# A hybrid attention, retention and mixture-of-experts layer: constants on the sync engine's queue, a twelfth weight buffer, x loaded first, two narrow rounding buffers for the last units, and the last 8 MB of weights by columns

## The reference

```python
h = rms_norm(x, norm1_g)
proj = h @ w_in                        # 2048 x 6736: q, k, v, index q/k/w, retention q/k/v/gate
attn_out = dsa_attention(...)          # an index score picks 64 keys a query, softmax over them
ret_out = silu(rg) * rms_norm(retention(rotate(rq), rotate(rk), rv))
x = x + concatenate([attn_out, ret_out]) @ w_out          # 2048 x 2048
h = rms_norm(x, norm2_g)
# router: the best of 4 groups, in it the best 2 of 8 experts, weights comb
a, b = h @ w1[e], h @ w3[e]            # for each of 32 experts, 2048 x 512
y = (silu(a) * b * comb[e]) @ w2[e]    # 512 x 2048
x = x + sum over e of y
```

## Time and profile before

| | |
|---|---|
| median of three runs | 1363.29 us |
| the profiled execution | 1364.37 us, of it 1362.5 us from the first to the last instruction |
| mean granted TensorE clock | 0.865 |
| TensorE busy | 985.4 us (72%) |
| VectorE, ScalarE, GpSimd busy | 330.6, 306.6, 80.0 us |
| moved by DMA | 480.69 MB, 353 GB/s over the span |
| chain that ended last | DMA 48%, TensorE 47%, VectorE 2% |

### The profile page before, as it was taken

How to read it: one execution, slowest core, us unless ns; L and a number is a source line. 1 busy time by engine, 2 the same in 40 slices (tenths; PEclk the granted TensorE clock), 3 DMA queues, 4 the chain that set the end, 5 groups by cost and what they waited for, 6 DMA issues and landing times.

```text
span 1362.5 us, 18965 instructions
## 1 busy us (share of the span) xinstructions
PE 985.4 (72%) x8264; PEld 654.3 (48%) x8264; DVE 330.6 (24%) x504; ACT 306.6 (23%) x553; POOL 80.0 (6%) x61
## 2 busy tenths in 40 slices
PE   7999999999999875556566365547736563674547
PEld 6987887888888651324234133313413421342222
DVE  5457967544753200010010000001001000100101
ACT  6545555555543310001001000100100010010000
POOL 1000242500110020000000000000000000000000
PEclk9999999999999888778787777888878777986888
DMA  8744644544596999999999999999999999999997
GB/s 278 231 153 158 213 145 137 183 164 147 192 411 237 405 426 435 430 426 431 432 432 425 436 431 427 433 431 433 424 435 432 426 434 432 429 425 435 430 423 305
DMA packets 61412, 480.69 MB, mean 353 GB/s; under 512 B 3816, under 2 KB 8096, under 8 KB 43952
## 3 DMA queue, kind: packets, MB, share of 16 engines
q1 hardware_dynamic: 60832, 478.89, 85.9%
q0 software_dynamic: 528, 1.06, 0.3%
HBM read 477.84 MB, written 2.10 MB: 352 GB/s over the span
## 4 chain that ended last, share of the span: by engine, by line
DMA 48%; PE 47%; DVE 2%; SPq 1%; issue 1%; ACT 1%; ACTq 0%
DMA ring<-w_dram 48%; PE ps L1559 11%; PE ps L1304 9%; PE ps L1306 9%; PE ps L1305 9%; PE ps L1597 5%; DVE w_lo L854 1%; PE ps L1514 1%; PE ps L1320 1%; DMA xs<-x_dram 1%; SPq L393 1%; PE ps L1661 1%; PE ps L1414 0%; PE ps L1336 0%; SPq L400 0%
## 5 line engine op out<-in xcount | busy, mean ns | idle before, releaser
L1559 PE MATMUL ps<-ring,side_buf 128*32 128x256 f32 x4000 | 273.5, 438 | 252.3 <-DMA ring<-w_dram 252.3
L1559 PEld LDWEIGHTS ps<-ring,side_buf 128*32 128x32 f32 x4000 | 155.9, 126 | 372.9 <-issue 316.1
L1304 PE MATMUL ps<-w_hi,zT_half 128*128 128x512 f32 (+2 forms) x576 | 221.7, 385 | 1.7 <-DVE w_lo L854 1.7
L1306 PE MATMUL ps<-w_hi,zT_half 128*128 128x512 f32 (+2 forms) x576 | 218.6, 379 | 0.0
L1305 PE MATMUL ps<-w_lo,zT_half 128*128 128x512 f32 (+2 forms) x576 | 218.5, 379 | 0.0
L854 DVE TENSOR_TENSOR w_lo<-raw_buf,w_hi 128x1024 fp32r<-128x1024 f32 (+2 forms) x144 | 182.0, 1281 | 142.7 <-ACT w_hi L574 142.0
L1597 PE MATMUL ps<-ring,side_buf 128*32 128x512 f32 x960 | 129.6, 701 | 97.5 <-DMA ring<-w_dram 97.2
L574 ACT CAST w_hi<-raw_buf 128x1024 fp32r<-128x1024 f32 (+2 forms) x144 | 143.6, 1016 | 107.5 <-PE ps L1306 101.4
L1230 DVE TENSOR_TENSOR xs<-xs,ps 128x512 f32<-128x512 f32 x56 | 38.5, 688 | 487.8 <-PE ps L1526 487.7
L792 ACT ACTIVATE side_buf<-ps,st 128x256 f32<-128x256 f32 x16 | 6.7, 470 | 554.2 <-PE ps L1559 554.2
L1597 PEld LDWEIGHTS ps<-ring,side_buf 128*32 128x32 f32 x960 | 35.8, 127 | 186.0 <-issue 179.5
(11 more groups left out here) (192 smaller groups left out, 501.3 us busy)
## 6 DMA issues: line engine op xcount, KB each, us to landing
ring<-w_dram SPq DMA_DIRECT2D x56, 4096.0 KB, 25.1
ring<-w_dram SPq DMA_DIRECT2D x73, 2048.0 KB, 21.4
raw_buf<-w_in_dram SPq DMA_DIRECT2D x48, 1024.0 KB, 5.0
raw_buf<-w_out_dram SPq DMA_DIRECT2D x16, 1024.0 KB, 6.0
spare<-w_dram SPq DMA_DIRECT2D x2, 2048.0 KB, 13.1
ring<-w_dram SPq DMA_DIRECT2D x4, 1024.0 KB, 14.0
ring<-w_dram SPq DMA_DIRECT2D x8, 512.0 KB, 17.4
raw_buf<-w_in_dram SPq DMA_DIRECT2D x4, 608.0 KB, 6.2
```

What stands on the lines that cost most here:

```text
L1304: mm(b, zhi(c)[:, t], wh, start=(c == 0), stop=False)
L1306: last = mm(b, zlo(c)[:, t], wh, start=False, stop=(c == C - 1))
L1559: last = mm(ps[part, up, pair * WIDE:(pair + 1) * WIDE], h_e[:, c, slots], w[m][:, cc * NB + h * WIDE:cc * NB + (h + 1) * WIDE], start=(c ...
```

## The change

- The gains, the constants and the router's weights are loaded by SP on its own queue: the first at q = 5, the router's at q = 63 behind a wait for `ret_ready`. GpSimd issues no DMA any more, and the 16 KB a partition that its queue had are a new tile `place`, a fourth extra buffer. It takes chunk 11 at q = 40.
- x: three of its four parts are loaded ahead of the first weights, and the first 1 MB of weights comes in two halves, with the last part of x between them. ScalarE and VectorE split one piece of x more ahead of the first unit.
- From unit 136 on (NARROW) only two slots of rounded weights are used, and a rounding waits for the unit before the last. The first spare area lies over the other two slots and takes chunk 9 when unit 135 has been used. The order of the loads behind the last raw weights changes, since `first_slot` does.
- The squares of block 2 move behind the last `copy_zT`; the sum of the squares moves behind `sel`; three products of 128 x 512 are added in front of the wait for `sel_ready`.
- The last four chunks come by columns: both rows of the left half, then each row of the right half. The left half is scattered ahead of the right half's products.

The diff, cut:

```diff
+NARROW = UNITS - 8
-RING, EXTRA = 8, 3
+RING, EXTRA = 8, 4
-LAST_PIECES = [(0, 0, 4), (1, 0, 2), (1, 2, 2)]
+LAST_PIECES = [(0, 2, 0, 2), (0, 1, 2, 2), (1, 1, 2, 2)]
+        w_split = nc.alloc_sbuf_tensor_at("w_split", [P, 8192], F32R, offset=side)
+        W_HI, W_LO = (4096, 0), (6144, 2048)
+        spare = [nc.alloc_sbuf_tensor_at(f"spare{i}", [P, 4096], F32, offset=side + 4 * 6144 * i) for i in range(2)]
+        place = sb("place", [P, 4096])
-        extra = [xs_flat, spare[0], spare[1]]
+        extra = [xs_flat, spare[0], spare[1], place[:, :]]
+        def split_slot(u):
+            return u % SPLIT if u < NARROW else u % 2
+        def split(part, u):
+            at = part[split_slot(u) // 2] + split_slot(u) % 2 * 1024
+            return w_split[:, at:at + 2 * unit(u)[2]]
@@ sync
-                if q == 1:
-                    for i in range(1, X_PARTS):
-                        load_x(i)
+                if q == 5:
+                    for dst, src in ((gain_q, q_norm_g), (gain_k, k_norm_g), (ln_w, idx_k_ln_w), (ln_b, idx_k_ln_b)):
+                        sp.dma_start(dst, src.partition_broadcast(P).rearrange("p l n -> p (l n)")).then_inc(gains_in, 16)
+                    sp.dma_start(gr_rows[:, :], ret_norm_g.rearrange("l (h d) -> (l h) d", d=HD)).then_inc(ret_gain_in, 16)
+                    sp.dma_start(const[:, P:CONSTS], consts[:, P:CONSTS]).then_inc(const_in, 16)
+                if q == 40:
+                    load_first(11)
+                if q == 63:
+                    sp.wait_ge(ret_ready, 2)
+                    sp.dma_start(g2_col[:, :], norm2_g.rearrange("l (p c) -> p (l c)", c=C)).then_inc(g2_in, 16)
...
+                    for g in range(GROUPS):
+                        sp.dma_start(stage_r[:, g].rearrange("p (q n) -> p q n", q=4),
+                                     w_router[0, g].rearrange("(q p c) e -> p q (c e)", q=4, c=4)).then_inc(router_in, 16)
+                if q == 0:
+                    load_x(1)
+                    load_x(2)
+                    sp.dma_start(at[:, 0:2 * n].rearrange("p (c n) -> p c n", c=2),
+                                 src[:, c:c + 2, col:col + n]).then_inc(raw_first, 16)
+                    load_x(3)
+                    sp.dma_start(at[:, 2 * n:4 * n].rearrange("p (c n) -> p c n", c=2),
+                                 src[:, c + 2:c + 4, col:col + n]).then_inc(raw_landed[0], 16)
...
+            sp.wait_ge(unit_used, NARROW)
+            load_first(9)
             sp.wait_ge(lo_done, UNITS - 4)
+            load_first(0)
+            sp.wait_ge(unit_used, UNITS - 4)
+            load_first(2)
+            sp.wait_ge(lo_done, UNITS)
             load_first(1)
-            sp.wait_ge(unit_used, UNITS - 4)
+            sp.wait_ge(unit_used, UNITS)
             load_first(3)
-            sp.wait_ge(lo_done, UNITS)
-            load_first(2)
-            sp.wait_ge(unit_used, UNITS)
-            load_first(4)
-            load_first(9)
             sp.wait_ge(logits_done, TH)
             sp.wait_ge(ssq_done, TH + 2 * OUT_BLOCKS)
             load_first(10)
@@ scalar
+                if u >= NARROW + 2:
+                    act.wait_ge(unit_used, u - 1)
+                elif u >= SPLIT:
                     act.wait_ge(unit_used, u - SPLIT + 1)
-                    if u == OUT_DONE[nb] + 4:
+                    if u == OUT_DONE[nb] + 4 and nb < OUT_BLOCKS - 2:
                         square_x2(nb)
             copy_zT(OUT_BLOCKS - 1)
+            square_x2(OUT_BLOCKS - 2)
             square_x2(OUT_BLOCKS - 1)
@@ tensor
+            for _ in range(3):
+                mm(ps[:, 0, :], ident, const[:, 0:NB], start=True, stop=True)
             pe.wait_ge(sel_ready, 1)
...
+                piece(0)
+                scatter_block(0)
+                scatter_block(1)
+                piece(1)
+                piece(2)
+                scatter_block(2)
+                scatter_block(3)
```

More of the change, by code:

```diff
@@ L448, in last_team @@
                     load(k, TEAMS - 1)
-                for i, (j, n, count) in enumerate(LAST_PIECES):
-                    at = j * D + n * NB
+                for i, (j, rows, n, count) in enumerate(LAST_PIECES):
                     for m in range(TEAM):
@@ L454, in last_team @@
                             sp.wait_ge(ring_used, it * TEAM_CHUNKS + (k - RING + 1))
-                        src = w2_v[(TEAMS - 1) * TEAM + m, 1]
-                        sp.dma_start(ring[:, chunk_slot(k), at:at + count * NB],
-                                     src[:, at:at + count * NB]).then_inc(piece_in[i], 16)
+                        src = w2_v[(TEAMS - 1) * TEAM + m, 1].rearrange("p (s n) -> p s n", s=2)
+                        dst = ring[:, chunk_slot(k), :].rearrange("p (s n) -> p s n", s=2)
+                        cols = slice(n * NB, (n + count) * NB)
+                        sp.dma_start(dst[:, j:j + rows, cols], src[:, j:j + rows, cols]).then_inc(piece_in[i], 16)
                 for n, count in STORES:
@@ L853, in rest_unit @@
                 v.wait_ge(hi_done, u + 1)
[L854 removed]
+                V.tensor_tensor(split(W_LO, u), raw(u), split(W_HI, u).bitcast(F32), ALU.subtract).then_inc(lo_done, 1)
             ik = proj[:, :, IK:IK + ID]
@@ L1642, in last_team, with piece @@
                 pe.wait_ge(gate_T_ready, it + 2)
-                for i, (j, n0, count) in enumerate(LAST_PIECES):
+                def piece(i):
+                    j0, rows, n0, count = LAST_PIECES[i]
                     pe.wait_ge(piece_in[i], 16 * TEAM)
                     for n in range(n0, n0 + count):
-                        for m in range(TEAM):
-                            part = slice(SLOTS * m, SLOTS * (m + 1))
-                            at = j * D + n * NB
-                            last = mm(ps[part, 4 + n, :], hm_lhsT(m, 2 + j),
-                                      ring[:, chunk_slot(LAST_GROUP + m), at:at + NB], start=False, stop=(j == 1))
-                        if j == 1:
-                            last.then_inc(y_whole, 1)
-                    if j == 0:
-                        continue
-                    for n in range(n0, n0 + count):
-                        pe.wait_ge(y_ready, it * 4 + (4 + n + 1))
-                        for th in range(TH):
-                            s = TH * n + th
-                            if s >= 2:
-                                pe.wait_ge(added, it * 8 + (16 + s - 1))
-                            mm(ps[:, 3 - s % 2, :], gate_T[:, th * P:(th + 1) * P], y_sb[:, n * NB:(n + 1) * NB],
-                               start=True, stop=True).then_inc(scattered, 1)
@@ new lines, in piece @@
+                        for j in range(j0, j0 + rows):
+                            for m in range(TEAM):
+                                part = slice(SLOTS * m, SLOTS * (m + 1))
+                                at = j * D + n * NB
+                                last = mm(ps[part, 4 + n, :], hm_lhsT(m, 2 + j),
+                                          ring[:, chunk_slot(LAST_GROUP + m), at:at + NB], start=False, stop=(j == 1))
+                        if j0 + rows == 2:
+                            last.then_inc(y_whole, 1)
@@ new lines, in scatter_block @@
+                def scatter_block(n):
+                    pe.wait_ge(y_ready, it * 4 + (4 + n + 1))
+                    for th in range(TH):
+                        s = TH * n + th
+                        if s >= 2:
+                            pe.wait_ge(added, it * 8 + (16 + s - 1))
+                        mm(ps[:, 3 - s % 2, :], gate_T[:, th * P:(th + 1) * P], y_sb[:, n * NB:(n + 1) * NB],
+                           start=True, stop=True).then_inc(scattered, 1)
+                piece(0)
```

72 lines of the change are left out of this document (31 added, 41 removed).

## The result

| | before | after |
|---|---|---|
| median | 1363.01 us (4 runs) | 1348.62 us (4 runs, 1347.60 to 1352.52) |
| profiled execution, its span | 1364.37, 1362.5 us | 1352.52, 1350.7 us |
| ratio of the times | | 0.9901, 95% interval 0.9888 to 0.9914 |

The changed kernel is 14.4 us faster. The profiled execution is the slowest of the four, and its span is only 1.1 us under the 1351.8 that I had worked out; the account further down says why that nearness is partly luck.

What follows compares the result with a forecast made beforehand. The second stage was taken as bound by its DMA stream at 429 GB/s. Stream -10.4 us (including earlier start and kept clock) and end -0.3 gave -10.7, from 1363.29 to 1352.6 us; 8-in-10 range 1350.3 to 1357.3.

Steps and rivals of the forecast that it cites:

- the sum for the stream: Second stage's chunk loads: five chunks fewer save 24.5 us, the stream starts 14.1 us later, net -10.4 us.
- The term of the start: Loading and transposing x: only pieces 6 and 7 remain, so the first unit starts 1.6 us earlier; bounds 0 and -3.4.
- The constants on SP's queue: Small loads moved from GpSimd to SP at q = 5 and q = 63: 0 us, with over 10 us of slack.
- the rival at q = 63: Seven small loads hold up SP's queue, later weights come late and TensorE stands: 1365.3 us, chance 0.04.
- The narrow buffers: Last units of the first stage: two slots of rounded weights just fit, 2.4 against 2.72 us a unit; 0 us.
- The bound of 14.5 us: Upper bound for two slots of rounded weights: six units with no overlap at all, 2.4 us each.
- The restart bound by ring_used: With twelve chunks in, the stream restarts after TensorE's first 64 products, ring_used at 457.4 us, with 180 chunks to go.
- The twelfth chunk's lead: Chunk 11, loaded at q = 40, is one of five chunks fewer in the stream, at 4.89 us each.
- The clock: Between the stages: three added products keep TensorE at 2.4 GHz, ring_used 2.3 us earlier; bounds -2.3 and +0.1.
- the rival with the falling clock: The clock falls all the same or the first group is late: ring_used at 459.8, 1355.0 us; chance 0.18.
- The end: Last four chunks by columns: 0.6 us gained, 0.3 lost to shorter 4 KB runs; together -0.3 us.

Runs made afterwards that it cites:

- the copy of the changed kernel: The changed kernel run once more without any edit, on one chip with the kernel before: 1348.97 us, ratio 0.9890 to before.
- the misaligned run: The changed kernel with 32 unused bytes in front of the ring, which then starts at 288 instead of 256: 1356.17 us, ratio 0.9946 to before.
- the wide buffers: The changed kernel with four slots of rounded weights to the end and chunk 9 loaded behind the last unit: 1351.65 us, ratio 0.9917 to before.
- the late chunk: The changed kernel with chunk 11 loaded after ring_used instead of at q = 40: 1355.00 us, ratio 0.9938 to before.
- the old start: The changed kernel with first weights ahead of three parts of x and no split piece in advance: 1352.32 us, ratio 0.9920 to before.

## Why the prediction was wrong, step by step

**The step that failed is the sum for the stream.** I priced five chunks fewer at 4.89 us each and took that price, the 429 GB/s of the earlier trace rows, for the 180 that are left too; a change of the rate had no term. Giving up the software queue's 16 KB moved the ring from byte 16512 to 256, from an odd multiple of 128 to a multiple of 256, and each packet became 4 ns shorter, 432 instead of 430 GB/s. From 500 to 1300 us the packets move 430.3 GB/s before and 432.2 after. 180 chunks of 2.097 MB take 877.3 us at the one rate and 873.4 at the other: 3.9 us by the packets, and 4.2 and 4.5 by the times of the two pairs of kernels that differ in the ring's start alone. With it the forecast of 1352.6 becomes 1348.1 to 1348.7, where 1348.6 and 1349.0 were measured. The edit was in the diff, as an argument and an allocation; I counted what it frees and not what it moves.

In the profiled executions other errors hid this one. The mean end of the DMA engines moved from 1348.2 to 1335.4 us, 12.7 us and not 10.4; but the slowest engine was 5.6 us behind it instead of 3.8, which gave 1.8 back, and the rest of the span became 0.9 shorter. So the span fell by 11.8, near the 10.7 of the forecast, and that is luck.

The Trainium skill (DMA: Bandwidth & Descriptors, "How a descriptor splits into AXI transactions") says that a descriptor which does not start at a multiple of 256 bytes begins with a transaction from the boundary below, and pays for the bytes in front. The runs agree that a start at a multiple of 256 is the better one, here on the side that is written, and show that the price is one for a packet, not by its size: +3.6 ns at 16 KB, +3.8 at 32 KB for 128 bytes off. They don't agree with a price by the bytes in front: 32 bytes off cost +4.6 and +4.9 ns, more than 128 bytes off. Why a packet takes longer is shown by no run.

**The term of the start** was -1.6. The two profiles show -2.1 (13.87 for 15.95 us), where pieces 6 and 7 took 1.09 us and not half of 3.45; in the copy of the changed kernel they took 1.97, and the first product came at 14.20. Over all traces it comes at 13.7 us on the mean with the new start (eight, 13.0 to 15.0) and at 15.5 with the old one (nine, 14.5 to 16.2): 1.8 us. It is passed on whole: in all 17 the last unit's load goes 427.0 to 427.5 us behind the first product. Undone, the start costs 3.3 us in the medians; the rest is open.

**The constants on SP's queue** were 0 and are 0. The kernel before with this edit alone took 1363.71 us, TensorE waits no longer in the changed kernel, and so the rival at q = 63 fell.

**The narrow buffers** were 0 for TensorE and are; what they give, chunk 9 in the idle time, is 2.7 us in the medians without them, and 0.7 in the trace. (The bound of 14.5 us for them is 6 x 2.4 = 14.4.)

**The restart bound by ring_used** held: 458.34 and 457.63 us for 457.4, with twelve chunks in. The twelfth chunk's lead was 4.9 us in the sum and cost 6.0 in the medians to undo, of which the trace shows 5.0 (882.2 us from ring_used to the mean end for 877.2).

**The clock** was taken as kept, and that step failed in part. Of the eight profiles with the added products it was kept in three, with ring_used 16.1 us behind the last unit's load, where the forecast had 16.0; in two it fell for some 3 us (17.2 us behind), and in three for some 6 (18.9), hardly better than the 19.3 without the products. Where it fell, they ran at 1.2 GHz themselves and held up the rank products (1.2 us in the first profile after). So the rival with the falling clock, which I had given 0.18, came true in five of eight, and the faster stream hid it in the time. Nor does all of it reach the end: in the copy of the changed kernel, with the clock kept, the first load on ring_used went some 3 us sooner than without the products, but the last weights landed only some 1 us sooner, both counted from the last unit's load (1339.67 less 441.51 and 1340.73 less 441.39 us).

**The end** was -0.3 and is 0 to -0.5 on the kernel before. Behind the last landing it is -0.7 to -0.9; what the slowest engine does ahead of it is larger than the term.

**Open:** single executions of the changed kernel spread from 1347.6 to 1352.5 us, those of before from 1362.2 to 1365.0, and the only two traces of the changed kernel are of executions of 1352.5 and 1351.1 us. What makes the slowest DMA engine 3 us late in one and 5.6 in another, and when the clock falls, isn't shown. 2 us of the misaligned run, 2 of the wide buffers', 1 of the late chunk's and 1 to 2 of the old start lie in this.

## What to carry to other kernels

Where an edit frees or adds memory ahead of a streamed buffer, work out the buffer's new address too: a ring that large packets are written to should start at a multiple of 256 bytes, and a padding of 128 bytes was worth 4.5 us of 1364 here, with packets of 16 and 32 KB. In a kernel bound by its stream, count the chunks that are left when the stream last runs without a gap, and what releases it then; each buffer filled in slack ahead of that is worth a chunk. A term measured with everything else equal between two profiles isn't safe until the rate of the long stretch has been compared too. And where the last landing ends the kernel, compare the mean end of the DMA engines beside the time: a single trace can be 2 us off by its slowest engine alone.

## What the runs showed of the hardware that I had not expected

- Packets of 16 KB took 611 ns and of 32 KB 1213 ns, nearly all the same, when the ring started at a multiple of 256 bytes, and mostly 611 to 622 and 1213 to 1225 ns when it started 128 bytes off; 611 to 621 and 1214 to 1224 when 32 bytes off, most often 614 and 1216.
- The use of the software queue by GpSimd made no difference to the packets of SP's queue (614.6 ns with it and without).
- The clock fell to 1.2 GHz at 445 us in one execution of the changed kernel and not at all in the next, with the same instructions: TensorE had done full products until 441, then transposes and products of 36 columns. Filling the wait that follows with three products of 128 x 512 kept it at 2.4 GHz in three of eight profiles.
- The slowest of the 16 DMA engines landed its last weights 3.0 to 5.6 us behind the mean end of all, in kernels whose long stream ran at the same 432 GB/s.
